# Another order of the work of one step in a gated delta net

## The reference, cut to what matters

```
state_t = a_t * state_(t-1) * (I - b_t k_t k_t^T) + b_t v_t k_t^T
o_t     = state_t q_t
```

```python
a_mat = where(strict, (kb @ k^T) * decay, 0)      # kb = k * beta, decay_ij = exp(g_i - g_j)
sol   = triangular_solve(I + a_mat, [v*beta, kb*exp(g)])
attn  = where(tril, (q @ k^T) * decay, 0)
def step(state, ...):                             # one chunk after the other
    v_new = u_i - w_i @ state
    o_i   = q_i @ state + attn_i @ v_new
    state = state * exp(gl_i) + k_i^T @ v_new
```

## Time and profile before

| | |
|---|---|
| median of 3 runs | 1445.21 us (1443.62 to 1445.22) |
| the profiled execution | 1439.3 us, its span 1437.6 us |
| busy, share of the span | PE 91%, PEld 77%, DVE 74%, ACT 60%, POOL 30% |
| delta net, 313 to 525 us | PE 180.3 us, DVE 141.8, ACT 119.3, POOL 130.9 busy of 212.0; granted clock 0.92 |

### The profile page before, as it was taken

How to read it: one execution, slowest core, us unless ns; L and a number is a source line. 1 busy time by engine, 2 the same in 40 slices (tenths; PEclk the granted TensorE clock), 3 DMA queues, 4 the chain that set the end, 5 groups by cost and what they waited for, 6 DMA issues and landing times. The chain is left out here.

```text
span 1437.6 us, 24617 instructions
## 1 busy us (share of the span) xinstructions
PE 1312.8 (91%) x8394; PEld 1107.2 (77%) x8394; DVE 1059.4 (74%) x1330; ACT 861.5 (60%) x1162; POOL 432.8 (30%) x473
## 2 busy tenths in 40 slices
PE   4999999978898979999964899999999999999994
PEld 3999778867787878668854688888888888888871
DVE  5895797775777758542137788888888888888847
ACT  7473445565555564552122577777777777777742
POOL 6020099018656737312201111111111111111130
PEclk9999999978999989999975999999999999999997
DMA  9174987411234139801124899999999999999865
GB/s 268 47 227 145 284 243 226 112 41 51 47 87 133 26 121 344 303 16 44 45 107 151 325 391 417 412 411 411 404 416 411 411 413 411 410 409 412 364 234 217
DMA packets 154680, 357.49 MB, mean 249 GB/s; under 512 B 43983, under 2 KB 100587, under 8 KB 127467
## 3 DMA queue, kind: packets, MB, share of 16 engines
q1 hardware_dynamic: 131755, 297.04, 55.3%
q0 software_dynamic: 14976, 40.43, 8.3%
q10 hardware_dynamic: 7872, 19.01, 3.4%
HBM read 287.64 MB, written 68.78 MB: 248 GB/s over the span
## 5 line engine op out<-in xcount | busy, mean ns | idle before, releaser
L2839 PE MATMUL gate_up_mm<-w_hi,gathered_T_hi 128*128 128x512 f32 x528 | 213.2, 404 | 7.8 <-DVE gathered_T_lo L3022 7.8
L2841 PE MATMUL gate_up_mm<-w_hi,gathered_T_lo 128*128 128x512 f32 x528 | 208.2, 394 | 0.0
L2840 PE MATMUL gate_up_mm<-w_lo,gathered_T_hi 128*128 128x512 f32 x528 | 207.8, 394 | 0.0
L3017 DVE TENSOR_TENSOR w_lo<-w_down,w_hi 128x2048 fp32r<-128x2048 f32 x66 | 148.5, 2289 | 54.6 <-ACT w_hi L2945 54.6
L2790 POOL COPY gather_idx<-slot_token 128x1 int32 (+1 forms) x34 | 25.9, 763 | 476.3 <-PE x_turned L2829 449.4
L3017 DVE TENSOR_TENSOR w_lo<-w_gate,w_hi 128x2048 fp32r<-128x2048 f32 x66 | 150.8, 2289 | 19.2 <-ACT w_hi L2945 18.1
L2945 ACT ACTIVATE w_hi<-w_gate 128x2048 fp32r<-128x2048 f32 x66 | 126.9, 1923 | 52.4 <-PE gate_up_mm L2841 31.5
L2945 ACT ACTIVATE w_hi<-w_up 128x2048 fp32r<-128x2048 f32 x66 | 126.7, 1923 | 49.9 <-PE down_mm L2876 49.9
L3017 DVE TENSOR_TENSOR w_lo<-w_up,w_hi 128x2048 fp32r<-128x2048 f32 x66 | 150.7, 2287 | 4.1 <-ACT w_hi L2945 0.5
L2945 ACT ACTIVATE w_hi<-w_down 128x2048 fp32r<-128x2048 f32 x66 | 125.1, 1918 | 40.7 <-issue 20.8
L2839 PEld LDWEIGHTS gate_up_mm<-w_hi,gathered_T_hi 128*128 128x128 f32 x528 | 100.8, 191 | 34.2 <-issue 11.9
(11 more groups left out here) (506 smaller groups left out, 3093.5 us busy)
## 6 DMA issues: line engine op xcount, KB each, us to landing
w_down<-in_expert_w_down SPq DMA_DIRECT2D x66, 1024.0 KB, 7.1
w_gate<-in_expert_w_gate SPq DMA_DIRECT2D x64, 1024.0 KB, 7.5
w_up<-in_expert_w_up SPq DMA_DIRECT2D x64, 1024.0 KB, 8.3
expert_rows_dram<-ones SPq DMA_DIRECT2D x32, 512.0 KB, 6.8
expert_rows_dram<-expert_out ACTq DMA_DIRECT2D x32, 512.0 KB, 8.6
x<-s_rows_dram SPq DMA_DIRECT2D x9, 1184.0 KB, 7.9
s_rows<-s_rows_dram SPq DMA_DIRECT2D x7, 1184.0 KB, 7.5
w_raw<-in_w_in SPq DMA_DIRECT2D x12, 512.0 KB, 5.3
```

The lines of the kernel that those rows point to most:

```text
L2839: pe.matmul(dst, xT_hi[:, k, :], hi[:, at, cols], start=k == 0, stop=False)
L2840: pe.matmul(dst, xT_hi[:, k, :], lo[:, at, cols], start=False, stop=False)
L2841: mm = pe.matmul(dst, xT_lo[:, k, :], hi[:, at, cols], start=False, stop=k == KT - 1)
L3017: dve.tensor_tensor(lo[:, at, :], flat(j), hi[:, at, :].bitcast(F32), ALU.subtract).then_inc(S["piece_lo"], 1)
```

## The change

Only the lists in `STEP_ORDER` are other ones. `delta_schedule`, all waits, all instructions and SP's order stay. On PE, `kq f 1, kq b 1` go from their place between `d5` and `turn5` to the end of the step, after `kk`; `read_q` goes after `turn4`, `z5` ahead of `solve`, and `d5` ahead of `attend`. DVE, ACT and POOL take their entries in the order that this gives: DVE does both `read_k` ahead of both `d4`, `d5` ahead of `attend`, and `kq` last; ACT does both `decay` between `vdec` and `turn5`; POOL does `add_o` ahead of `spread_tt`. The order of `z6` and `d6`, both directions in turn, is the same before and after.

```diff
 STEP_ORDER = {
-    "PE": "z4 f 0, z4 b 0, read_k f -1, read_k b -1, d4 f 0, d4 b 0, read_q f -1, read_q b -1, turn4 f 0, turn4 b 0, "
-          "solve f -1, solve b -1, z5 f 0, z5 b 0, attend f -1, attend b -1, d5 f 0, d5 b 0, kq f 1, kq b 1, "
-          "turn5 f 0, turn5 b 0, new_state f -1, new_state b -1, z6 f 0, kk f 2, kk b 2, d6 f 0",
-    "DVE": "read_k f -1, d4 f 0, read_k b -1, d4 b 0, base f 1, attend f -1, attend b -1, d5 f 0, d5 b 0, kq f 1, "
-           "kq b 1, new_state f -1, new_state b -1, kk f 2, kk b 2",
-    "ACT": "z4 f 0, z4 b 0, read_q f -1, turn4 f 0, turn4 b 0, solve f -1, solve b -1, z5 f 0, z5 b 0, read_q b -1, "
-           "vdec f -1, vdec b -1, turn5 f 0, turn5 b 0, decay f 2, z6 f 0, z6 b 0, decay b 2, d6 f 0, d6 b 0",
-    "POOL": "alev4 f 1, alev4 b 1, vb f 0, vb b 0, mask f 1, mask b 1, alev5 f 1, alev5 b 1, spread_tt f 1, "
-            "spread_tt b 1, spread_t f 1, spread_t b 1, add_o f -1, add_o b -1",
+    "PE": "z4 f 0, z4 b 0, read_k f -1, read_k b -1, d4 f 0, d4 b 0, turn4 f 0, turn4 b 0, read_q f -1, read_q "
+          "b -1, z5 f 0, z5 b 0, solve f -1, solve b -1, d5 f 0, d5 b 0, attend f -1, attend b -1, turn5 f 0, "
+          "turn5 b 0, new_state f -1, new_state b -1, z6 f 0, kk f 2, kk b 2, kq f 1, kq b 1, d6 f 0",
+    "DVE": "read_k f -1, read_k b -1, d4 f 0, d4 b 0, base f 1, d5 f 0, d5 b 0, attend f -1, attend b -1, "
+           "new_state f -1, new_state b -1, kk f 2, kk b 2, kq f 1, kq b 1",
+    "ACT": "z4 f 0, z4 b 0, turn4 f 0, turn4 b 0, read_q f -1, read_q b -1, z5 f 0, z5 b 0, solve f -1, solve b "
+           "-1, vdec f -1, vdec b -1, decay f 2, decay b 2, turn5 f 0, turn5 b 0, z6 f 0, z6 b 0, d6 f 0, d6 b 0",
+    "POOL": "alev4 f 1, alev4 b 1, vb f 0, vb b 0, mask f 1, mask b 1, alev5 f 1, alev5 b 1, add_o f -1, add_o b "
+            "-1, spread_tt f 1, spread_tt b 1, spread_t f 1, spread_t b 1",
 }
```

## The result

The changed kernel took 1450.06 us in the median of 20 runs (1444.4 to 1454.28), the kernel before 1446.44 us in 20 runs on the same chip (1441.32 to 1452.51). The ratio is 1.0028, with a 95% interval of 1.0017 to 1.004: slower by 3.6 us in the medians and about 4 us by the ratio, well under 2%. The forecast was +1.25 us, 1446.4 us and "same".

A forecast was written before the change was run, and what follows sets the result against it. A loop of waits through DVE's inversion, no engine full, bounds the delta net step. +1.7 + 5 x (24.7 - 24.96) - 0.45 + 0.9 + 0.4 = +1.25 on 1445.2 gives 1446.4 us, range 1443 to 1449.5.

The forecast's parts named there:

- `z6` held by ACT: PE ahead of `z6`: idle 1.6 us until R+17.3, as ACT does both `decay` before the `turn5` copies.
- long step, full clock: A delta net step with the change, from one first DVE `read_k` (R) to the next: 24.7 us.
- step 0: First delta net step: `kq` now runs behind `z6` instead of while ACT is on its way, +1.7 us.
- five long steps: The five alike delta net steps: 24.7 us each against a mean of 24.96 before, 5 x (24.7 - 24.96).
- step 6, step 7, tail: Delta net's end: POOL's `spread_tt` sets step 6, -0.45; `turn4` stall in step 7, +0.9; ACT's `read_q` in tail, +0.4.
- the clock in the sum: PE's clock over the new idle stretches: 0 taken for falls, though one fall costs 1.64 us.
- 10 us of slack: `decay` loads on SP's queue: they follow the blocks and have 10 us to spare.
- Costs nothing: POOL's moves, `add_o` ahead of `spread_tt`: no cost as long as `z6` is late; otherwise `spread_tt` next, 1 us behind.
- The clock falls at the new stretches: Slower rival, ahead of `z6` or `turn4`: 1.64 us a fall, up to +11.5, 1450 to 1458 us; chance 0.22.
- ACT does not hold `z6`: Faster rival: ACT reaches `turn5` 1.6 us earlier, step 23.1 us, 8 us less, 1438.5 us; chance 0.11.
- PE is the bound: Faster rival: only PE's 21.1 us of products a step count, 19 us less, 1427 us; chance 0.02.
- The profiled run had few falls: Rival: timed runs before fall in all six steps, none after; 3.3 us below forecast, 1443.1 us; chance 0.10.

The follow-up runs named there:

- first profile of before: The kernel before, unchanged, in the profile the prediction was made from: 1439.3 us, delta net stretch 211.26 us.
- the second profile: The kernel before, unchanged, profiled again on this chip: 1431.12 us, delta net stretch 207.66 us.
- the filled kernel: Changed kernel with unread products added on PE, 12 ahead of `z6` and 6 ahead of `turn4`: 1445.76 us, 1.0026 of the kernel before.
- the repaired one: Changed kernel with ACT's old order, `turn5` copies ahead of both `decay`: 1428.68 us, 0.9931 of the kernel before.
- the first experiment: Changed kernel with ACT's old order of `turn5` and `decay` restored: 1428.68 us, 0.9931 of the kernel before.

## Why the prediction came out as it did

The waits came where the prediction put them, and "same" and the range held. The size did not: about +4 us for +1.25. What each place was charted at, and what the first profiles show (the last three rows are differences from before):

| step of the prediction | charted | measured |
|---|---|---|
| idle ahead of `turn4` | 1.25 + 0.4 | 1.03 + 0.23 |
| idle ahead of `turn5` | 0.65 | none in step 1 (inversion 7.15 us, not 8.3) |
| `z6` held by ACT | 1.6, at R+17.3 | 1.83, at R+16.9 |
| long step, full clock | 24.7 | 24.18 |
| step 0 | +1.7 | +2.75 |
| five long steps | -1.3 | +0.85 against the first profile of before, +6.5 against the second |
| step 6, step 7, tail | -0.45, +0.9, +0.4 | 0.0, +1.55, +0.27 |

*What failed is the clock in the sum, and with it the base of the long steps.* The prediction put the new step without a fall (24.7) against the mean of the old one with its falls (24.96), though it had itself worked out 23.6 for the old one undisturbed. That 23.6 is what the second profile shows (23.52 to 23.60). Like for like the order costs +0.6 us a step (24.18 - 23.57), and the chart would have given +1.1. Taking the clock at 0 falls for the new order was wrong as well: both its profiles have four, each in step 0, in one of steps 1 to 3, in step 4 and after step 6's wait.

Over the profiles the stage was 207.7, 211.3 and 218.5 us before, and 216.7 and 217.3 after; the means differ by 4.5 us. By places that is +2.8 in step 0 (charted +1.7), +0.3 in the five long steps together (-1.3), -0.3 in step 6 (-0.45), +1.5 in step 7 (+0.9) and +0.3 in the tail (+0.4). The misses of step 0 and step 7 are the falls: without one step 7 is 18.46, +0.9 as charted, and step 0, in the filled kernel, 36.15 or +1.2. The fall in step 0 the prediction had named as possible and left out of the sum. That these means lie close to the 4 us timed may be luck, as the three profiles of before spread over 10.8 us. That the total came out near the forecast is partly luck too: the charted long step was 0.5 us too long, which paid for part of the falls and of the late load.

*The cover of the `decay` loads.* "10 us of slack" failed in step 4: behind the three large rows on SP's queue the row came 1.39 us late, `z6` waited 3.32 us instead of 1.83 and a fall followed. That step is 27.3 us against 24.9, and filling did not mend it (27.03).

*POOL's `add_o`.* "Costs nothing" holds in step 5, as said, since `z6` is late there. In step 6, where there is no `decay` to hold `z6`, the forecast had `spread_tt` set the step and so was near (24.02 for 23.6). Its chart of POOL has `add_o` in it, but the move was given no price: without it the step is 21.6.

*The rivals.* "The clock falls at the new stretches" came true in part, with four falls of the up to seven that it reckoned with; whether it made the change slower is open, since taking the falls away in the profile moved neither kernel's times beyond their intervals. The idle stretches that the prediction compared by length do not decide by themselves: falls came behind 1.83 us (in one of steps 1 to 3) and behind 1.95 to 1.99 (step 0), and in other steps the same 1.83 us had none.

The Trainium skill's page "TensorE: Matmul & The Clock Gate", section "HAM oscillation — how this bites in real kernels", has the clock fall in every turn of a loop, behind waits of about 3 to 5 us. The traces agree where the waits are that long: behind the 3.56 us of the old order with `kq` moved it fell in all six steps, and behind the 4.21 to 4.24 us of a late inversion each time. Behind the usual 2.56 us of the old order, and behind the 1.83 us of the new one, it fell in some turns only; the page's example says nothing of waits as short as these.

"ACT does not hold `z6`" is false for the changed kernel. It is true of the repaired one, by the place of ACT's entries and not because ACT was faster than charted. "PE is the bound" is false: PE is busy 21.1 us of 24.18, and changing two places on ACT, which is busy 14, took off 1.89. "The profiled run had few falls" is not borne out: the first profile had four, the others one and five, and the new order has falls of its own.

So the change has two parts of opposite sign. All moves but that of the `decay` gain 1.3 us a step together (23.57 to 22.29), shown by the first experiment; what each of them gives was not run, except that `kq` moved alone loses. The two `decay` ahead of `turn5` lose 1.83 to 1.89 of it, shown by the same experiment and by the old schedule, where that order is free. `add_o` ahead of `spread_tt` loses another 2.4 us once, in the profile of step 6. Open stays how often the clock falls and the inversion is late in the timed executions, and what that costs there.

## What to carry to other kernels

Put a new schedule's undisturbed step against the old one's, or mean against mean over several profiles, but never one against the other; several profiles of the same kernel also show the noise of the base. When entries of an in-order list are moved, ask of every list which entry another engine waits for next, and let nothing that can be done later (here `decay`, `add_o`) stand ahead of it. An order that is free in one schedule can cost its full length in the next, when the gap that covered it is closed.

## What the runs showed of the hardware

- The clock's falls differ between executions of one program: one, four or five of six steps of the kernel before. The granted clock was then 0.51 (1.2 GHz) for some 3.5 us, at times for 6.8. Counted over the profiles, steps 1 to 6 of the old order had one behind 6 of 18 idle stretches of 2.56 to 2.82 us, behind 6 of 6 of 3.56 and 6 of 6 of 4.21 to 4.24. The changed order with ACT's new list had one behind 3 of 12 of 1.82 to 1.87 us ahead of `z6`, behind 3 of 3 of 3.32 to 3.41 in step 4, and behind 3 of 3 of 1.95 to 1.99 in step 0.
- A PE instruction of a 32-bit product that moves 64 columns through a full 128 by 128 weight takes 0.114 us, about as much as one of 128 columns (0.118, 1.89 us for 16); those of the earlier trace rows with 128*64 take 0.034.
- DVE's inversion takes 7.15 us in the changed kernel and 7.6 to 8.3 in the old order with the usual gap (up to 10 where it is late), with the same instructions. The difference lies in those with POOL at work beside them: in step 5 of before against step 1 of after, L1003 takes 1.47 us against 1.03, L1010 0.62 against 0.38, the first copy 0.87 against 0.38, and POOL's second `mask` took 2.07 against 1.29. In the new order POOL is idle from the first copy on until `attend`. That this is the cause was not tried by itself.
